# Softmax weights divided on ScalarE, and LayerNorm's sums on TensorE, in a two-layer decoder trunk on one core

## The reference

```
p = jax.nn.softmax(s, axis=-1)                   # 8 heads, 256 queries, causal keys, head size 128
o = p @ v

y32 = (y + conv_b)                               # 1024 channels, after a causal convolution of 31 taps
mu = mean(y32, axis=-1)
var = mean(square(y32 - mu), axis=-1)
y32 = (y32 - mu) * rsqrt(var + EPS) * ln_g + ln_b
out = silu(y32)
```

## Time and profile before

| | us |
|---|---|
| runs shown | 988.69, 989.47, 984.85 |
| their median | 988.69 |
| the profiled execution | 985.91 |
| its span in the trace | 984.1 |
| TensorE busy | 940.6 |
| VectorE busy | 822.2 |
| ScalarE busy | 423.0 |
| GpSimd busy | 72.8 |

### The profile page before, as it was taken

How to read it: one execution, slowest core, us unless ns; L and a number is a source line. 1 busy time by engine, 2 the same in 40 slices (tenths; PEclk the granted TensorE clock), 3 DMA queues, 4 the chain that set the end, 5 groups by cost and what they waited for, 6 DMA issues and landing times.

```text
span 984.1 us, 18714 instructions
## 1 busy us (share of the span) xinstructions
PE 940.6 (96%) x7024; PEld 906.8 (92%) x7024; DVE 822.2 (84%) x1238; ACT 423.0 (43%) x726; POOL 72.8 (7%) x86
## 2 busy tenths in 40 slices
PE   2998999999999999999999999999998989999998
PEld 2887889999999999999999999999998989998887
DVE  5886858987999779889888999888999987878964
ACT  2310125444565444433544544444554655744331
POOL 1000000010110000122200000000030102000000
PEclk9998999999999999999999999999999999999999
DMA  9999878888876878999958655544445456588962
GB/s 361 409 409 409 323 268 319 318 318 342 324 277 249 297 258 306 329 357 353 352 188 305 207 173 190 175 151 143 158 164 179 171 173 214 193 313 283 364 222 78
DMA packets 75618, 261.26 MB, mean 265 GB/s; under 512 B 7952, under 2 KB 8592, under 8 KB 75296
## 3 DMA queue, kind: packets, MB, share of 16 engines
q1 hardware_dynamic: 70336, 240.90, 68.2%
q10 hardware_dynamic: 2880, 10.49, 2.7%
q0 software_dynamic: 2336, 8.98, 2.4%
HBM read 256.07 MB, written 4.19 MB: 264 GB/s over the span
## 4 chain that ended last, share of the span: by engine, by line
PE 68%; DVE 20%; DMA 7%; issue 2%; ACT 2%; SPq 1%; DVEq 0%; ACTq 0%
PE bank L844 12%; PE bank L846 11%; PE bank L845 11%; DVE acc L1219 7%; DVE wlo L1209 6%; PE bank L902 4%; PE bank L989 4%; PE bank L991 4%; PE bank L992 4%; DMA Y<-ada_units 4%; PE bank L865 3%; DVE Y L1436 3%; DMA ada<-ada_units 2%; PE bank L936 2%; PE bank L863 2%
## 5 line engine op out<-in xcount | busy, mean ns | idle before, releaser
L503 ACT ACTIVATE whi<-raw 128x1024 fp32r<-128x1024 f32 x256 | 270.1, 1060 | 378.1 <-PE bank L846 202.8
L1209 DVE TENSOR_TENSOR wlo<-raw,whi 128x1024 fp32r<-128x1024 f32 x256 | 312.2, 1234 | 72.9 <-ACT whi L503 71.9
L844 PE MATMUL bank<-hhi,whi 128*128 128x256 f32 x912 | 262.5, 288 | 1.7 <-ACT T L750 0.9
L845 PE MATMUL bank<-hlo,whi 128*128 128x256 f32 x912 | 258.7, 284 | 0.0
L846 PE MATMUL bank<-hhi,wlo 128*128 128x256 f32 x912 | 258.6, 284 | 0.0
L1219 DVE SCALAR_TENSOR_TENSOR acc<-ada,cact,acc 128x1024 f32<-128x1024 f32 x152 | 198.7, 1307 | 24.7 <-DMA ada<-ada_units 17.5
L844 PEld LDWEIGHTS bank<-hhi,whi 128*128 128x128 f32 x912 | 175.5, 192 | 4.3 <-issue 3.1
L845 PEld LDWEIGHTS bank<-hlo,whi 128*128 128x128 f32 x912 | 175.7, 193 | 0.1
L846 PEld LDWEIGHTS bank<-hhi,wlo 128*128 128x128 f32 x912 | 175.6, 193 | 0.0
L989 PE MATMUL bank<-whi,hhi 128*128 128x256 f32 x512 | 147.5, 288 | 1.0 <-DVE wlo L1209 1.0
L992 PE MATMUL bank<-wlo,hhi 128*128 128x256 f32 x512 | 145.6, 284 | 0.0
(11 more groups left out here) (203 smaller groups left out, 1214.0 us busy)
## 6 DMA issues: line engine op xcount, KB each, us to landing
raw<-w_slabs SPq DMA_DIRECT2D x260, 512.0 KB, 4.5
ada<-ada_units SPq DMA_DIRECT2D x160, 512.0 KB, 6.7
raw<-w_slabs ACTq DMA_DIRECT2D x20, 512.0 KB, 7.1
V<-ada_units SPq DMA_DIRECT2D x16, 512.0 KB, 9.8
Y<-ada_units SPq DMA_DIRECT2D x16, 512.0 KB, 10.8
X<-xT SPq DMA_DIRECT2D x1, 2048.0 KB, 12.5
x_dram<-X POOLq DMA_DIRECT2D x4, 512.0 KB, 7.4
outT<-X POOLq DMA_DIRECT2D x3, 512.0 KB, 5.4
```

What stands on the lines that cost most here:

```text
L503: act.activation(whi[:, slot], raw[:, slot], ACT.Copy).then_inc(hi_done, 1)
L844: mm(out, whi[:, s, k, :], ahi[:, c, :], start=(c == 0), stop=False)
L845: mm(out, whi[:, s, k, :], alo[:, c, :], start=False, stop=False)
L1209: dve.tensor_tensor(wlo[:, s], source, whi[:, s].bitcast(F32), ALU.subtract)\
```

## The change

The division leaves VectorE: `divide` on VectorE becomes `invert`, which takes the reciprocal only and signals a new semaphore, `sum_inv`. It moves from behind the first `lo` to the start of the step. ScalarE gets a `divide` of two in-place copies with the reciprocal as scale; it is called behind `hi` (both halves) and ahead of the eviction, for the same head in the same step as before.

GpSimd's sums for LayerNorm go, with the tiles `means` and `spreads` and the semaphores `mean_part` and `var_part`. TensorE multiplies ones by all eight chunks for the mean, and takes the sums of all eight chunks of squares, one behind each of the first eight chunks of slab 113, where three stood behind the slab. GpSimd keeps the sums of x's squares in layer 0.

```diff
-            def add_conv(j):
-                pool.wait_ge(conv_seq, 2 * CONV_WIDTH * (j // 2 + 1))
-                if j == 1:
-                    own(pool.tensor_tensor(means, Y[:, 0, :], Y[:, 1, :], ALU.add))
-                else:
-                    own(pool.tensor_tensor(means, means, Y[:, j, :], ALU.add))
...
-            slopes(1, range(0, 2))
-            for j in range(1, HC - 2):
-                add_conv(j)
-            pool.sem_inc(mean_part, 1)
-            slopes(1, range(2, HC))
-            pool.wait_ge(ln_sq, 1)
-            own(pool.tensor_tensor(spreads, U[:, 0, 0:SEQ], U[:, 1, 0:SEQ], ALU.add))
-            for j in range(2, HC - 2):
-                own(pool.tensor_tensor(spreads, spreads, U[:, j, 0:SEQ], ALU.add))
-            pool.sem_inc(var_part, 1)
+            slopes(1)
...
+            def divide(layer, i):
+                if 0 <= i < HC:
+                    a = HC * layer + i
+                    act.wait_ge(sum_inv, a + 1)
+                    for q, (c0, c1) in enumerate(((0, P), (P, KEYS))):
+                        act.activation(SP[:, a % 2, c0:c1], SP[:, a % 2, c0:c1], ACT.Copy,
+                                       scale=rl[:, a % 2, q:q + 1]).then_inc(p_scaled, 1)
...
                 hi(w + AHEAD, None)
+                divide(0, w - V0 - 4)
...
                 hi(w + AHEAD, None)
+                divide(1, w - V1 - 4)
...
                     pe.wait_ge(ln_sq, 1)
-                    slab(w, None, hhi, hlo)
-                    by_token(XB, U[:, HC - 2, 0:SEQ], True, False)
-                    by_token(XB, U[:, HC - 1, 0:SEQ], False, False)
-                    pe.wait_ge(var_part, 1)
-                    by_token(XB, spreads, False, True).then_inc(var_mm, 1)
+                    slab(w, None, hhi, hlo, between=lambda c: c < HC and
+                         by_token(XB, U[:, c, 0:SEQ], c == 0, c == HC - 1))
+                    pe.sem_inc(var_mm, 1)
...
                     pe.wait_ge(conv_seq, N_TAPS)
-                    pe.wait_ge(mean_part, 1)
-                    mm(XB[:, 0:SEQ], ones[:], means, start=True, stop=False)
-                    for j in range(HC - 2, HC):
-                        ins = mm(XB[:, 0:SEQ], ones[:], Y[:, j, :], start=False, stop=(j == HC - 1))
+                    for j in range(HC):
+                        ins = mm(XB[:, 0:SEQ], ones[:], Y[:, j, :], start=(j == 0), stop=(j == HC - 1))
                     ins.then_inc(mean_mm, 1)
...
-            def divide(layer, i):
+            def invert(layer, i):
                 if 0 <= i < HC:
-                    a = HC * layer + i
-                    dve.wait_ge(exp_done, 2 * (a + 1))
-                    seq(dve.reciprocal(rl[:, i % 2, :], ls[:, i % 2, :]))
-                    settle()
-                    for q, (c0, c1) in enumerate(((0, P), (P, KEYS))):
-                        ins = dve.tensor_scalar(SP[:, i % 2, c0:c1], SP[:, i % 2, c0:c1], rl[:, i % 2, q:q + 1],
-                                                None, ALU.mult)
-                        ins.then_inc(p_scaled, 1)
+                    dve.wait_ge(exp_done, 2 * (HC * layer + i + 1))
+                    dve.reciprocal(rl[:, i % 2, :], ls[:, i % 2, :]).then_inc(sum_inv, 1)
...
                 i = w - v0 - 3
+                invert(layer, i - 1)
                 lo(w + AHEAD, None, (0,))
-                divide(layer, i - 1)
```

More of the change, by code:

```diff
@@ L155, in build @@
         squares = SP[:, 0, 0:SEQ]
-        means, spreads = QI[:, 0, :], QI[:, 1, :]
         VX = V[:].rearrange("p a (b t) -> p (a b) t", t=SEQ)
@@ L206, in build @@
         ds_ready, scored, s_added, max_done = sem("ds_ready"), sem("scored"), sem("s_added"), sem("max_done")
+        sum_inv = sem("sum_inv")
         exp_done, p_scaled, pt_done, pt_copied = sem("exp_done"), sem("p_scaled"), sem("pt_done"), sem("pt_copied")
@@ L213, in build @@
         conv_seq = sem("conv_seq")
-        mean_part, var_part = sem("mean_part"), sem("var_part")
         mean_mm, ln_sub, ln_sq, var_mm = sem("mean_mm"), sem("ln_sub"), sem("ln_sq"), sem("var_mm")
```

## The result

| | us |
|---|---|
| changed kernel, median of 4 runs | 1001.21 (999.13 to 1003.1) |
| before, median of 4 runs | 986.95 (984.85 to 989.47) |
| ratio | 1.014, 95% interval 1.0121 to 1.0158 |
| profiled execution and its span | 999.13, 997.3 |

A forecast was written before the change was run, and what follows sets the result against it. TensorE, busy in 96% of the span, was taken as the bound. 985.9 + 11.6 (division) + 4.4 (LayerNorm sums) = 1001.9 us, plus 0.6, stated as 1002.5; range 996 to 1009, 8 in 10 within 994 to 1012.

The forecast's parts named there:

- The order of the queues: Attention steps: ScalarE's copies stand behind its second rounding, released at TensorE's slab end; weight transposes wait 1.41 us.
- part one: Division moved to ScalarE: 22.4 us of new waits, less 9.3 of old waits and 1.5 of slow clock, +11.6 us.
- the seventh head's: Seventh step behind each layer's first: no key transposes (0.21 us), so TensorE comes earlier and waits 1.62 us.
- the 0.18 us off each wait: Attention waits: each costs 0.18 us less than its length, read from a 0.58 us wait that cost 0.40.
- The first head of layer 1: Second layer's first head: ScalarE late, both roundings back to back, so a wait of 2.2 us, 2.0 in cost.
- The slow clock behind it: Granted clock of 0.50 after the old kernel's longest wait, 1.5 us lost; taken as gone with a shorter wait.
- Part two's products: LayerNorm's sums on TensorE: mean's five more products +2.15 us, dealt-out squares +2.3 us, together +4.4 us.
- VectorE's relief: VectorE's convolution without GpSimd's additions beside it: gain of 0 to 1.2 us, taken as 0.
- The sum: Whole kernel: 985.9 + 11.6 + 4.4 = 1001.9 us against the profiled execution; 1002.5 us stated after adding 0.6.
- (a): Rival, attention: new waits bring TensorE's clock down, 1.5 us a drop, on half of 16 steps 12 us: 1014; 12%.
- (b): Rival, weight transposes: ScalarE's copies ready before TensorE asks, old waits and slow clock go: 979.5 us; 5%.
- (c): Rival, attention steps: half of each wait covered, about 0.6 us a step, dealt-out squares free: 988 us; 6%.

The follow-up runs named there:

- moving the one call: Changed kernel with ScalarE's division called between its two roundings of a step instead of behind both: 977.82 us against 985.1, ratio 0.9919.
- its second measurement: Kernel before with only the division moved to ScalarE, LayerNorm's sums still shared with GpSimd, measured once more: 998.94 us against 986.96, ratio 1.0129.
- the division alone: Kernel before with only the division moved to ScalarE, LayerNorm's sums still shared with GpSimd: first measured 1000.8 us against 985.1, ratio 1.0155.
- the kernel with one extra pair: Changed kernel, two more copies on ScalarE ahead of its division: 1015.96 us, ratio 1.0288; with squares as a block behind slab 113: 1016.91 us, ratio 1.03.
- the run with the relief alone: Kernel before without GpSimd's ten LayerNorm additions and nothing in their place (result not the reference): 981.76 us against 985.8, ratio 0.9955.

## Why the prediction was right, point by point

- **The order of the queues decides part one: right, and shown** by moving the one call. A full step's wait was worked out as 1.41 us and is 1.42; the pair of copies 0.79 and 0.78; the seventh head's 1.62 and 1.64; the last head's 2.17 and 2.10 in layer 0, 2.38 in layer 1. The forecast period of 8.85 us is the measured one, 1.24 us over 7.61 for a wait of 1.42, so the 0.18 us off each wait was right too.
- **Part one's total: right.** 11.6 us forecast; 12.0 by the trace of that part alone and 12.0 by its second measurement.
- **The first head of layer 1: wrong for the changed kernel, right for the division alone.** I had taken 2.2 us from VectorE's and ScalarE's lateness in the trace of before; it is 2.17 with GpSimd's additions and 1.42 without them, since the change itself takes that lateness away. The slow clock behind it went, as forecast.
- **Part two's products: nearly right.** Line 1169's 16 loads take 1.19 + 2.13 = 3.3 us, 2.15 more than before as forecast; the squares' chunks stand 0.80 us apart, which with 0.36 for a chunk's three products of 0.12 is 0.44 each, 0.11 an instruction as forecast. Slab 113 grew by 2.2 us where I had said 2.3. What was off is the price in a block, which I had read as 0.10 from eight starts. All 32 as a block, in the kernel with one extra pair, take 854.96 - 851.38 = 3.58 us, 0.11 each as well, so dealing them out costs nothing at the full clock and hides nothing:

```profile
851.38 3.66 PEld L910 LDWEIGHTS bank<-ones,U 128*128 128x128 f32 x32
854.96 0.30 PEld L1031 LDWEIGHTS bank<-PTs,V 128*128 128x128 f32 x2
```

- **VectorE's relief: the step that failed.** I took it as 0, with a bound of 1.2 us, since "in attention the waits are already counted as gone". But in the changed kernel ScalarE's division still hangs on VectorE through the exponential, which waits for VectorE's maximum: the first exponential of layer 1 waited 2.10 us for it in the division alone, and 0.86 in the changed kernel. The relief took 0.75 us off the first head's wait and the 1.2 us ahead of it. By itself, in the kernel before, it is worth 4.0 us (0.9955). While GpSimd adds, six taps of the convolution have a median of 838 ns and a longest of 1041; the same six taps in the changed kernel:

```profile
L1419 DVE SCALAR_TENSOR_TENSOR Y<-U,par,Y x6: 471/473/721, 728.2 to 731.1; 128x256 f32<-128x256 f32 x6
```

The longest, 721 ns, falls beside GpSimd's slope products, which both kernels have. So part two cost 2.4 us behind the new division instead of 4.4, and nothing with the old one; this is a difference of two medians whose intervals overlap, and the stages give 2.3. The rule of the Trainium skill that I had weighed as saying "the move would pay" (GPSIMD Engine Reference, 1. Specifications) deserved more weight than I gave it: the trace (838 and 473 ns) and the run with the relief alone (4.0 us) agree with it.

- **The sum: right, by 1.7 us too high.** 16.0 against 14.3. The relief accounts for 2.0 us, which I had put at nothing; part one was 0.4 too low. The number came out close because this term was small beside the division's 12 us.
- **The rivals.** (a) The clock did not fall in the attentions of the changed kernel. That it can fall behind such waits was right: with waits of 2.33 us and more it often did, and once, with the division alone, it fell behind one of 2.10, a length that the changed kernel has too. So a drop in some of its executions isn't excluded. The rule that I had named for this from the Trainium skill (TensorE: Matmul & The Clock Gate, Part 1) agrees with these drops. (b) The faster side was a matter of one line of code: the condition I had named, copies done before TensorE asks, is what the moved call meets. Its price was 979.5 us, 6.4 under the profiled execution; measured were 7.3 under before, with two waits left and VectorE's relief on top, which nearly cancel. (c) Nothing spoke for it.

## What to carry to other kernels

Before work is moved to an engine with spare time, find the instruction ahead of it in that engine's queue and ask what releases it: behind an instruction that waits for the bound engine, even idle time can't be used, and the result comes late by the length of everything between. With LayerNorm's sums left alone, the same copies one place earlier turned 12 us lost into 6 us won. And an engine that is not the bound (VectorE here) can still be on the path in one short stretch, so that what slows it there (GpSimd beside it) has a price that its average share hides.

## What the hardware showed that I had not expected

- The length of a wait does not decide alone whether TensorE's clock falls to 0.50 around its end. In all traces together: 2.11 us, none of 24; 2.10, one of four; 2.33, three of four; 2.38, none of four; 2.79, three of four; 2.80, two of twelve; 3.02, none of two; 3.48, both. In the kernel before, the wait of 3.05 had a drop and the one of 2.86 had none.
- In both traces where the clock fell ahead of the slab with one-column products dealt out between its own, it stayed at 0.50 for 16 us with TensorE busy all the time. Most drops behind attention waits ended within 4 us, one took about 6.5.
- A one-column fp32 product costs 0.11 us an instruction at the full clock, between the products of a slab as well as in a block: dealing it out hides nothing.
